# Second attention with the values as weights, probabilities divided before the product, and work ordered by pairs of tiles

## The reference

```python
h  = modulate(rms_norm(x), sh1, sc1)            # context tokens likewise
q_a, k_a, v_a, q_b, k_b, v_b = split(h @ w_in)  # 8 heads of 64 in each of two groups
# group a: window of 128 + 256 context keys + one sink column per head (k, v shared by 4 heads)
p   = softmax(concat([s_loc, s_ctx, sink]))
o_a = p_loc @ v + p_ctx @ v_ctx
# group b: neighbourhood with a bias table + 256 context keys, no sink
o_b = softmax(concat([s_loc + bias, s_ctx])) @ concat([v, v_ctx])
merged = concat([rms_norm(o_a) * on_a, rms_norm(o_b) * on_b]) @ w_out
x = x + g1 * merged
x = x + g2 * ((silu(h2 @ w_gate) * (h2 @ w_up)) @ w_down)    # h2 = modulate(rms_norm(x), sh2, sc2)
```

## Time and profile before

| | us |
|---|---|
| median of 3 runs | 907.43 (907.34 to 909.88) |
| the profiled execution | 908.71 |
| its span in the profile | 906.9 |
| TensorE busy in it | 831.2 (92%) |
| VectorE / ScalarE / GpSimd busy | 391.3 / 254.6 / 48.8 |
| attention loop, first scores to the last turn | 598.35 to 673.6 |
| from there to the first MLP matmul | to 708.18 |
| `up_first` | to 728.1 |

### The profile page before, as it was taken

One profiled execution on the slowest core, in us unless ns is written; L12 is line 12 of the kernel. 1 busy time (PEld: TensorE's weight loads), 2 busy tenths in 40 slices (PEclk: granted clock), 3 DMA queues, 4 the chain that ended last, 5 costly groups with the idle time before them and its releaser, 6 DMA issues.

```text
span 906.9 us, 12924 instructions
## 1 busy us (share of the span) xinstructions
PE 831.2 (92%) x5263; PEld 580.6 (64%) x5263; DVE 391.3 (43%) x718; ACT 254.6 (28%) x410; POOL 48.8 (5%) x33
## 2 busy tenths in 40 slices
PE   8999999989988978788678699889999999999998
PEld 6877767766564555255245254377874788888886
DVE  1457154435452111101101356762433675765765
ACT  2252213431032212112112211134542343433431
POOL 1000041101000000000000002500000000000000
PEclk9999999989999997999899999989999999999999
DMA  9952546569678999999999995410000734645501
GB/s 330 314 200 96 184 182 235 186 208 346 228 249 298 408 405 405 409 405 405 405 408 405 400 314 185 134 53 1 2 1 6 273 139 162 244 150 178 194 1 47
DMA packets 124058, 208.40 MB, mean 230 GB/s; under 512 B 7625, under 2 KB 42730, under 8 KB 123890
## 3 DMA queue, kind: packets, MB, share of 16 engines
q1 hardware_dynamic: 121138, 203.52, 61.1%
q10 hardware_dynamic: 2816, 4.27, 1.5%
q0 software_dynamic: 64, 0.05, 0.0%
HBM read 206.74 MB, written 1.08 MB: 229 GB/s over the span
## 4 chain that ended last, share of the span: by engine, by line
PE 72%; DMA 11%; DVE 7%; SPq 4%; issue 3%; ACT 1%; POOL 1%; ACTq 0%; DVEq 0%; POOLq 0%
PE psa L513 8%; DMA arena<-in_w_down_dram 7%; PE psv L1092 5%; PE psa L1092 4%; PE psa L919 4%; PE psa L990 3%; PE psx L1015 3%; PE psa L864 3%; DMA arena<-in_w_in_dram 3%; SPq L374 2%; PE psa L749 2%; PE psa L852 2%; PE psv L1093 2%; PE psa L1093 2%; PE psx L540 2%
## 5 line engine op out<-in xcount | busy, mean ns | idle before, releaser
L2127 DVE TENSOR_TENSOR unit_parts<-ring,unit_parts 128x2048 fp32r<-128x2048 f32 x33 | 75.5, 2289 | 59.2 <-ACT unit_parts L1517 59.2
L1517 ACT ACTIVATE unit_parts<-ring 128x2048 fp32r<-128x2048 f32 x33 | 63.2, 1914 | 74.8 <-PE psa L1093 43.8
L513 PE MATMUL psa<-arena,ring 128*128 128x256 f32 x320 | 69.9, 380 | 1.0 <-ACT arena L1286 1.0
L1092 PE MATMUL psv<-column_parts,unit_parts 128*128 128x512 f32 (+1 forms) x192 | 66.9, 397 | 2.5 <-DVE arena L2154 1.4
L513 PEld LDWEIGHTS psa<-arena,ring 128*128 128x128 f32 x320 | 60.6, 190 | 10.3 <-DVE arena L1580 1.2
L1092 PE MATMUL psa<-column_parts,unit_parts 128*128 128x512 f32 (+1 forms) x192 | 65.5, 389 | 0.0
L919 PE MATMUL psa<-ring,arena 128*128 128x512 f32 (+1 forms) x160 | 62.1, 550 | 0.8 <-DVE arena L1678 0.8
L876 PE MATMUL psv<-ring,arena 128*32 128x256 f32 x1024 | 57.3, 380 | 0.5 <-DMA ring<-in_w_up_dram 0.5
L1093 PE MATMUL psv<-column_parts,unit_parts 128*128 128x256 f32 (+1 forms) x192 | 52.7, 274 | 0.0
L1093 PE MATMUL psa<-column_parts,unit_parts 128*128 128x256 f32 (+1 forms) x192 | 52.1, 271 | 0.0
L919 PEld LDWEIGHTS psa<-ring,arena 128*128 128x128 f32 x160 | 30.3, 190 | 32.6 <-issue 30.1
(11 more groups left out here) (376 smaller groups left out, 1421.7 us busy)
## 6 DMA issues: line engine op xcount, KB each, us to landing
ring<-in_w_gate_dram SPq DMA_DIRECT2D x43, 1024.0 KB, 9.3
ring<-in_w_up_dram SPq DMA_DIRECT2D x43, 1024.0 KB, 5.2
arena<-in_w_down_dram SPq DMA_DIRECT2D x32, 1024.0 KB
ring<-in_w_in_dram SPq DMA_DIRECT2D x24, 1024.0 KB, 10.1
ring<-in_w_mod_dram SPq DMA_DIRECT2D x24, 1024.0 KB, 7.4
ring<-in_w_down_dram SPq DMA_DIRECT2D x11, 1024.0 KB, 7.3
ring<-in_w_out_dram SPq DMA_DIRECT2D x8, 1024.0 KB, 6.1
arena<-in_w_in_dram SPq DMA_DIRECT2D x8, 512.0 KB, 12.2
```

Of the source, the lines that this page charges most:

```text
L513: mm = pe.matmul(bank[:, cc * T:(cc + 1) * T], w, hT[:, k, :], start=(k == 0), stop=(k == KD - 1))
L1092: pe.matmul(both_parts(bank, t_0, t_1), hi, col_parts[:, :, k, t_0:t_1], start=(k == 0), stop=False)
L1517: act.activation(unit_parts[q % 3][:, 0, :], slot_of(NPRE + u_), ACT.Copy).then_inc(upper_done, 1)
L2127: vec.tensor_tensor(lo, slot_of(NPRE + at["mlp"] + 3 * n + kind), hi, ALU.subtract).then_inc(lower_done, 1)
```

## The change

- In `values2` the values (128 keys x 64 columns) are the weights and the turned probabilities move through (128 columns). The result stands with head dimensions on the partitions: even heads on 0 to 63, odd heads on 64 to 127, four column blocks a group. The two heads of a pair are interleaved matmul by matmul. The heads of group a are paired anew (`PAIRS_A`), so that a pair has both one head of each key group and one even and one odd head. The order on TensorE is now scores, values, turns.
- Before the turn, VectorE divides the exponentials: `norm_probs` adds the sink's exponential (group a), takes the reciprocal and multiplies the 128x512 tile in place. ScalarE makes the sink's exponential for each tile of group a (128x1).
- The loops of VectorE and ScalarE go by pairs of tiles. For every eight tiles ScalarE squares the result, VectorE adds the squares of the four column blocks and writes `oT` with the gains, straight out of PSUM (`outputs`). The transposes of the attention outputs and their copies are gone, and the division, the multiplication and the squares of the old tail with them.
- The sums over the head dimensions come from a matmul with ones (`square_sums`). The norm's factor, one number for each token and group, is applied after the projection: `project_out` makes a sum for each group in a bank of its own, and `add_attention` does for each `(sum x factor) x gate` and then adds, so twice as many instructions.
- Half (0,0) of the projection is put into the loop: group a's part after the turns of pair 14, group b's part before the last `values2`. Three MLP units are split by ScalarE at the start of the tail; `lower(0)` and `lower(1)` on VectorE stand before and after `add_attention(0, 0)`.

```diff
+PAIRS_A = (0, 5, 1, 4, 2, 7, 3, 6)
...
-                  for h in ((0, 4, 1, 5, 2, 6, 3, 7) if kind == 0 else range(8))]
+                  for h in (PAIRS_A if kind == 0 else range(8))]
...
             def turn2(n):
-                pe.wait_ge(exps2_done, n + 1)
+                pe.wait_ge(probs2_normed, n + 1)
...
-                for m in range(4):
-                    mm = pe.matmul(bank[:, h * HD:(h + 1) * HD], PT2[:, n % 4, m * P:(m + 1) * P], vs[m],
-                                   start=(m == 0), stop=(m == 3))
+                    r0, c0 = HD * (h % 2), P * (h // 2)
...
+                    steps.append([(PSX[n // 8 % 2][r0:r0 + HD, c0:c0 + P], vs[m], PT2[:, n % 4, m * P:(m + 1) * P])
+                                  for m in range(4)])
+                for m, two in enumerate(zip(*steps)):
+                    for o_, l_, r_ in two:
+                        mm = pe.matmul(o_, l_, r_, start=(m == 0), stop=(m == 3))
+                        if m == 3:
+                            mm.then_inc(values2_done, 1)
...
+            def project_out(b, half, kinds=(0, 1)):
+                for kind in kinds:
+                    for k in range(4 * kind, 4 * kind + 4):
+                        mm = pe.matmul(halves[b, half][kind][:], oT[:, k, b * P:(b + 1) * P],
+                                       out_units[2 * half + k // 4][:, k % 4, :], start=(k % 4 == 0), stop=(k % 4 == 3))
+                    mm.then_inc(halves_ready, 1)
...
             for p in range(NT // 2 + 2):
                 if p < NT // 2:
                     scores2(p)
+                if p >= 2:
+                    if p == NT // 2 + 1:
+                        project_out(0, 0, (1,))
+                    values2(p - 2)
                 if 1 <= p <= NT // 2:
                     turn2(2 * p - 2)
                     turn2(2 * p - 1)
-                if p >= 2:
-                    values2(2 * p - 4)
-                    values2(2 * p - 3)
+                if p == NT // 2 - 1:
+                    pe.wait_ge(values2_copied, 2)
+                    pe.wait_ge(exps2_done, NT - 2)
+                    project_out(0, 0, (0,))
...
+            def square_sums(k):
+                pe.wait_ge(values2_copied, k + 1)
+                pe.matmul(PSX[0][:, 2 * k:2 * k + 2], sqs[:, k, :], c("ones")[:, 0:2],
+                          start=True, stop=True).then_inc(sums2_ready, 1)
+
+            for k in range(3):
+                square_sums(k)
+            project_out(0, 1)
+            pe.wait_ge(power_req, HEAD_POWERS[0])
+            square_sums(3)
+            project_out(1, 0)
...
             pe.wait_ge(rows_normed, 5)
-            turn_block(onat, 0)
...
             turn_block(hnx, 0)
...
+            pe.wait_ge(power_req, HEAD_POWERS[1])
             project_out(1, 1)
```

ScalarE:

```diff
+            def exps2(n):
+                act.wait_ge(max2_done, n + 1)
+                b, kind, h = tiles2[n]
+                if kind == 0:
+                    act.activation(den[:, stat(n):stat(n) + 1], sink[:, h:h + 1], ACT.Exp,
+                                   bias=nm2[:, stat(n):stat(n) + 1]).then_inc(sink_exp_done, 1)
...
+            for p in range(NT // 2 + 3):
+                if p < NT // 2:
+                    exps2(2 * p)
+                    exps2(2 * p + 1)
+                if p % 4 == 2 and p > 4:
+                    head_squares(p // 4 - 1)
+                if 1 <= p <= NT // 2:
+                    probs2(2 * p - 2)
+                    probs2(2 * p - 1)
...
             act.wait_ge(values2_done, NT)
-            act.wait_ge(heads_squared, 2 * NB)
-            upper(0)
+            for q in range(3):
+                upper(q)
```

VectorE:

```diff
+            def norm_probs(n):
...
+                if kind == 0:
+                    link(vec.tensor_tensor(total, total, den[:, j:j + 1], ALU.add))
+                link(vec.reciprocal(total, total))
+                vec.tensor_scalar(E2[:, n % 4, :], E2[:, n % 4, :], total, None, ALU.mult).then_inc(probs2_normed, 1)
+
             def outputs(k):
...
+                dve.wait_ge(heads_squared, k + 1)
+                vec.tensor_reduce(sqs[:, k, :], sqo[:, k % 2, :, :].rearrange("p c t -> p t c"), AX, ALU.add)
+                for cc in range(4):
+                    row = ROWS["on_a"] + 4 * kind + cc
+                    ins = vec.tensor_scalar(oT[:, 4 * kind + cc, b * P:(b + 1) * P], PSX[k % 2][:, cc * P:(cc + 1) * P],
+                                            vc[:, row:row + 1], None, ALU.mult)
+                ins.then_inc(values2_copied, 1)
...
+            for p in range(NT // 2 + 3):
+                if p < NT // 2:
+                    max2(2 * p)
+                    max2(2 * p + 1)
+                    norm_probs(2 * p)
+                    norm_probs(2 * p + 1)
+                if p % 4 == 2 and p > 4:
+                    outputs(p // 4 - 1)
+            head_norm(0)
+            lower(0)
...
+                    link(vec.scalar_tensor_tensor(tm, at["halves"][b, half][kind][:], rs5[:, 2 * b + kind:2 * b + kind + 1], gate,
+                                                  ALU.mult, ALU.mult))
...
             add_attention(0, 0)
-            turned_block(oT, 1, vc[:, ROWS["on_a"]:ROWS["on_a"] + KD])
+            lower(1)
             add_attention(0, 1)
+            head_norm(1)
             normed_block(0)
             add_attention(1, 0)
             turned_block(h3T, 0, modA[:, 2, :], modT[:, 24:32, 0])
             split_columns(0)
-            lower(0)
             add_attention(1, 1)
             normed_block(1)
-            lower(1)
```

More of the change, by code:

```diff
@@ new lines, in _ @@
+            out_units = [unit2(nu2 + m) for m in range(4)]
+            nu2 += 4
+            halves = {(0, 0): (SB[0], SB[1]), (0, 1): (PSV[(nv + 2) % 3], PSV[nv % 3]),
+                      (1, 0): (PSV[(nv + 1) % 3], SB[2]), (1, 1): (PSX[0], PSX[1])}
+            at["halves"] = halves
+            def project_out(b, half, kinds=(0, 1)):
[4 more added lines that the diff above has]
+                    mm.then_inc(halves_ready, 1)
@@ new lines, in head_norm, with lower @@
+            def head_norm(b):
+                nonlocal nrs
+                dve.wait_ge(sums2_ready, 3 + b)
+                nrs += 1
+                assert nrs == HEAD_POWERS[b]
+                vec.tensor_scalar(rs5[:, 2 * b:2 * b + 2], PSX[0][:, 4 * b:4 * b + 4].rearrange("p (k c) -> p k c", c=2)[:, :, 0],
+                                  1.0 / 512, EPS, ALU.mult, ALU.add).then_inc(power_req, 1)
+            def lower(q):
+                dve.wait_ge(upper_done, q + 1)
+                kind, n = mlp[q]
+                hi, lo = (unit_parts[q % 3][:, m, :] for m in range(2))
+                vec.tensor_tensor(lo, slot_of(NPRE + at["mlp"] + 3 * n + kind), hi, ALU.subtract).then_inc(lower_done, 1)
@@ new lines, in max2 @@
+            def max2(n):
+                b, kind, h = tiles2[n]
+                j = stat(n)
+                dve.wait_ge(scores2_done, n + 1)
+                src = at["SB"][n % 4][:]
+                if kind == 0:
+                    link(vec.tensor_reduce(mxt[:, n % 2:n % 2 + 1], src, AX, ALU.max))
+                    vec.tensor_scalar(nm2[:, j:j + 1], mxt[:, n % 2:n % 2 + 1], sink[:, h:h + 1], -1.0,
+                                      ALU.max, ALU.mult).then_inc(max2_done, 1)
+                else:
+                    vec.tensor_reduce(nm2[:, j:j + 1], src, AX, ALU.max, negate=True).then_inc(max2_done, 1)
@@ new lines, in _, with add_attention @@
+            for p in range(NT // 2 + 3):
[8 more added lines that the diff above has]
+            lower(0)
+            def add_attention(b, half):
+                xv = xres[:, b, half * 512:half * 512 + 512]
+                gate = gbc[:, 0, half * 512:half * 512 + 512]
+                for kind in range(2):
+                    m = 4 * b + 2 * half + kind
+                    dve.wait_ge(halves_ready, m + 1)
+                    if m % 4 == 0:
+                        dve.wait_ge(power_done, HEAD_POWERS[b])
+                    if m >= 2:
+                        dve.wait_ge(halves_added, m - 1)
+                    tm = (t0, t1)[kind]
+                    link(vec.scalar_tensor_tensor(tm, at["halves"][b, half][kind][:], rs5[:, 2 * b + kind:2 * b + kind + 1], gate,
+                                                  ALU.mult, ALU.mult))
+                    if m > 0:
+                        dve.wait_ge(halves_added, m)
+                    vec.tensor_tensor(xv, xv, tm, ALU.add).then_inc(halves_added, 1)
```

193 lines of the change are left out of this document (46 added, 147 removed).

## The result

| | before | after |
|---|---|---|
| median of 4 runs each, same chip | 908.39 us (907.34 to 909.88) | 899.01 us (897.40 to 899.54) |
| profiled execution (its span) | 908.71 (906.9) | 898.64 (896.8) |

The ratio is 0.9893, interval 0.9871 to 0.9914: 9.4 us faster, where 12.4 was forecast. First the page of the kernel after: the span, and each engine's busy time.

A forecast was written before the change was run, and what follows sets the result against it. TensorE was taken to bound the loop. Gains of 6.2 in the loop, 3.1 in the tail and 3.1 in `up_first` sum to 12.4 us, median 907.43 to 895.0; likeliest case 892 to 900, stated range 891 to 903.5.

The forecast's parts named there:

- TensorE stays the bound of the loop: Attention loop: TensorE sets the pace, 3.95 us a pair in group a and 4.35 in group b, 0.73 less each.
- The product: Values product in the loop: 1.10 us a pair, with 0.89 and 1.30 as bounds, against 1.83 before.
- the forecast's sign: Expected in the trace: values records of either head starting together, 0.11 to 0.14 us apart, 1.1 a pair.
- The chain of VectorE and ScalarE: Loop, group a: turns need 3.85 us against TensorE's 3.95; a rival had this bounding the loop, 902, chance 0.17.
- The start: Loop's first pairs: TensorE waits 2.8 us for the first divisions and copies; 1.6 lost after offsets.
- pair 10: `outputs` in group a, where little slack hides VectorE's extra work: 1.0 us lost in the loop.
- The sum of `outputs`: VectorE's addition of the squares in the loop, priced like a maximum: 0.6 to 0.7 us.
- The tail: From the last scores to `up_first`: 35.5 us instead of 38.6, so 3.1 gained.
- The wait for the rows: Ahead of `up_first`, TensorE waits 0.8 us for VectorE's normalised rows.
- The moved half of the projection: Projection (0,0): costs what it cost, covers the last division, turn and copy; some 2 us of copies ahead are gone.
- `up_first`: First MLP stage: 16.8 us instead of 19.9, 3.1 gained, of which 1.1 the wait for `lower(1)` and 1.6 the clock.
- The slower rival, the clock: Loop: waits make the clock fall to 0.50 repeatedly; 10 falls cost 16 us, giving 911; chance 0.05.

The follow-up runs named there:

- the last experiment: Kernel after with `outputs` and squares two pairs later, packed squares, `lower(0)` behind `add_attention(0, 0)`, `lower(1)` behind `head_norm(1)`: 895.02 us, ratio 0.9855.

## Why the prediction was right, and where its sizes were off

- **TensorE stays the bound of the loop: right.** Periods 3.97 and 4.37, forecast 3.95 and 4.35. The forecast gave 0.73 less a pair; the traces have 0.70 (4.67 and 5.07 in the earlier trace rows): the product came out 0.08 cheaper than forecast and the turns 0.09 dearer. Over 12 periods that is some 0.4 of the 0.6 that the loop fell short; the `outputs` are the rest (1.2 for 1.0).
- **The product: right, a little dear.** 1.03 against 1.10. The value comes from the two heads running side by side: both start a record every 0.11, the forecast's sign. Issued one after the other they overlap in part (1.51). The Trainium skill, "TensorE: Matmul & The Clock Gate", section "Part 3: Packing small matmuls", lets a weight load overlap a running matmul only in another row group. This trace doesn't agree: both heads use all rows, each record has a weight load of its own, and 16 records fit in 1.03 with loads under way in 0.85 of it.
- **The chain of VectorE and ScalarE: the right verdict from the wrong quantity.** I summed its latency, 3.85, and gave it a margin of 0.1. What decides is VectorE's own time a pair: 0.4 more and it is full, and every further microsecond counts in full. The latency counts where the loop starts and where something is put in.
- **The start (2.8) and pair 10 (1.0): right.** 2.59 and 1.10, or 1.2 by the run that moved them. The sum of `outputs` was priced like a contiguous maximum, 0.6 to 0.7, and takes 1.03.
- **The tail: the mis-sized term.** The wait for the rows was forecast as 0.8 and is 1.60. The step said that `head_norm` and GpSimd's power lie under the projection; the power was priced at what it takes alone. `lower(0)` beside it makes it 2.69, and VectorE waits 0.68 for it on the way to the rows: that is nearly all of the 0.80. With `lower` moved the whole wait goes, but there a subtraction is out of the way as well. What else the tail holds was forecast 0.5 too dear.
- **The moved half of the projection: right about what it covers, wrong about its worth.** It covers 2.5 us of waiting; without it the stretch is 0.83 longer and the time unchanged. I had not asked which wait is next when TensorE comes later.
- **`up_first`: right in its cause, 0.6 too much.** No wait for `lower`, a clock of 1.00. The gate of block 0 took 4.21 (700.76 to 705.69 less the wait; forecast 3.85 "as now", but the earlier trace rows have 4.20: 708.18 to 713.04 less the wait), the turns and the up unit of block 0 took 4.74 (forecast 4.75), block 1 7.59 (710.63 to 719.60 less the wait; forecast 7.35 and 0.2 for a drain), and 0.20 came as a wait for the columns. Of the 2.5 gained, the early units alone bring all in the kernel before.
- **The slower rival, the clock: didn't come.** 1.00 over the whole loop, in spite of the waits at its start and at the `outputs`. After a wait of 2.05 in `up_first`, in the run with `lower` moved, it did fall to 0.50.

Of the 3.0 between the gain forecast (12.4) and that of the medians (9.4), 1.6 lies in the terms above; the rest is how executions differ, 0.9 of it in the start of the attention and 0.7 in that the two profiled ones lie further apart than the medians (10.1), less the 0.2 behind the first `up`.

## What to carry to other kernels

Where a product has few weight columns, put two of them in different column halves of the array and issue their records in turns, and see in the trace that both halves start together. Of a move that fills a wait, ask which wait is next: here 2.5 us filled were worth 0.8. Moving work earlier on an engine is paid for by what stands behind it there: two early subtractions brought 3.05 in `up_first` and cost 1.8 ahead of it. And look at what a long VectorE instruction lies beside: here a GpSimd step of 0.7 us became one of 2.7.

## What the runs showed of the hardware

- GpSimd's 128x2 power takes 0.70 us, and 2.69 beside VectorE's 128x2048 subtraction of two tiles in SBUF. It starts 0.16 behind the subtraction's start and ends 0.57 behind its end, and the subtraction takes 2.28 or 2.29 either way. The Trainium skill, "SBUF — State Buffer", section "🔬 SBUF: two separate sides", tells of a port pair that such a VectorE instruction and a GpSimd instruction that reads SBUF hold one at a time, whoever comes first; the traces agree where VectorE came first, here and in the last experiment (2.67, with 0.55 behind the subtraction's end); no case here has GpSimd first.
- Distance between neighbours in SBUF costs on either engine: VectorE's sum over four values 512 B apart takes 1.03 us, over four adjacent ones 0.69; ScalarE's write of 512 values takes 0.59 in a row and 1.10 at a distance of 16 B.
- Two heads' products in different column halves (128x64 weights, 128 columns moving, fp32) start a record each every 0.11 us, as one head does alone.
- VectorE's 128x512 multiplication is listed with 0.48 or 0.49, but the next instruction starts 0.40 behind it; the 0.40 is what fills the engine.
